# Token halves inside the passes: the order of the token-stationary matrix products in a four-layer model kernel

## What is computed

```
x = first_block(x, ...)    # 2 layers: three mixers, then an expert layer (PEER, 16384 experts)
  u   = rms_norm(x) @ w_in                       # 1024 -> 3462 columns
  x   = x + concat(hgrn2, dilated attention, mamba2) @ w_out
  q   = rms_norm(x) @ w_query
  x   = x + sum over the chosen experts of gate * gelu(down @ x) * up
x = second_block(x, mem, ...)   # 2 layers
  p   = rms_norm(x) @ w_in_2                     # 1024 -> 5888 columns
  x   = x + (gated sum of conv @ w_a_out, retention @ w_b_out, gating @ w_c_out) @ w_o
  x   = x + cross_attention(rms_norm(x), mem; xa_q, xa_k, xa_v, xa_o)
  x   = x + (silu(h @ w1) * (h @ w3)) @ w2       # 2816 inner columns
return rms_norm(x) * final_norm
```

## Time and profile before

| | |
|---|---|
| median of 3 runs | 3015.52 us |
| lowest and highest | 3012.93 and 3020.16 us |
| span of the profiled execution | 3015.1 us |
| mean granted TensorE clock, of full speed | 0.991 |
| TensorE matmul busy | 2947.5 us, 98% of the span |
| VectorE busy | 2016.0 us, 67% |
| ScalarE busy | 1456.8 us, 48% |
| mean DMA rate | 175 GB/s |

### The profile page before, as it was taken

One profiled execution on the slowest core, in us unless ns is written; L12 is line 12 of the kernel. 1 busy time (PEld: TensorE's weight loads), 2 busy tenths in 40 slices (PEclk: granted clock), 3 DMA queues, 4 the chain that ended last, 5 costly groups with the idle time before them and its releaser, 6 DMA issues.

```text
span 3015.1 us, 43968 instructions
## 1 busy us (share of the span) xinstructions
PE 2947.5 (98%) x17320; PEld 2604.2 (86%) x17320; DVE 2016.0 (67%) x3109; ACT 1456.8 (48%) x2275; POOL 14.9 (0%) x37
## 2 busy tenths in 40 slices
PE   8989999999999999999999999999999999999998
PEld 6878888889999788888888999988898998888996
DVE  5859998765555686889885655547665556665554
ACT  5531775554444444157645444435455444545443
POOL 0000000000000000000000000000000000000000
PEclk9999999999999999999999999999999999999999
DMA  5334446775545433444568554546555656554563
GB/s 178 109 113 153 168 168 209 249 268 183 195 178 181 136 99 112 148 163 169 200 224 292 193 196 169 197 141 181 179 171 169 189 187 186 170 182 146 150 187 125
DMA packets 223246, 528.52 MB, mean 175 GB/s; under 512 B 13450, under 2 KB 87344, under 8 KB 212080
## 3 DMA queue, kind: packets, MB, share of 16 engines
q1 hardware_dynamic: 221856, 521.11, 52.1%
q0 software_dynamic: 1232, 5.25, 0.5%
HBM read 507.42 MB, written 18.88 MB: 175 GB/s over the span
## 4 chain that ended last, share of the span: by engine, by line
PE 93%; DVE 4%; ACT 2%; DMA 1%; issue 0%; SPq 0%; POOL 0%; DVEq 0%; ACTq 0%; POOLq 0%
PE ps L2211 16%; PE ps L1232 14%; PE ps L2195 12%; PE ps L1282 12%; PE ps L1295 12%; PE ps L1266 11%; PE ps L559 4%; PE ps L550 3%; PE ps L1221 2%; PE ps L2452 1%; PE ps L653 1%; PE ps L1047 1%; DVE ring_lo L533 0%; PE ps L2376 0%; PE ps L2360 0%; PE ps L1207 0%
## 5 line engine op out<-in xcount | busy, mean ns | idle before, releaser
L1869 DVE TENSOR_TENSOR ring_lo<-ring,w_hi 128x1024 fp32r<-128x1024 f32 x320 | 388.8, 1224 | 272.2 <-ACT w_hi L1865 270.9
L1865 ACT ACTIVATE w_hi<-ring 128x1024 fp32r<-128x1024 f32 x320 | 336.7, 1057 | 270.5 <-PE ps L2211 183.9
L1232 PE MATMUL ps<-h_t,ring 128*128 128x256 f32 x2048 | 463.8, 379 | 1.1 <-ACT arena L882 0.9
L1232 PEld LDWEIGHTS ps<-h_t,ring 128*128 128x128 f32 x2048 | 378.9, 190 | 48.1 <-issue 1.3
L1282 PE MATMUL ps<-h_t_lo,down_hi 128*128 128x256 f32 x1024 | 288.2, 281 | 0.0
L1282 PE MATMUL ps<-h_t_expert,down_lo 128*128 128x256 f32 x1024 | 287.8, 281 | 0.0
L1282 PE MATMUL ps<-h_t_expert,down_hi 128*128 128x256 f32 x1024 | 286.8, 280 | 0.0
L2195 PE MATMUL ps<-h_t_hi,w_hi 128*128 128x256 f32 x928 | 259.9, 280 | 2.7 <-ACT arena L2010 2.7
L2195 PE MATMUL ps<-h_t_lo,w_hi 128*128 128x256 f32 x928 | 261.5, 282 | 0.0
L2195 PE MATMUL ps<-h_t_hi,ring_lo 128*128 128x256 f32 x928 | 259.7, 280 | 0.0
L1656 DVE TENSOR_TENSOR up_lo<-ring,up_hi 128x2048 fp32r<-128x2048 f32 x64 | 146.7, 2292 | 101.4 <-ACT up_hi L945 101.4
(11 more groups left out here) (442 smaller groups left out, 6700.2 us busy)
## 6 DMA issues: line engine op xcount, KB each, us to landing
ring<-in_peer_down SPq DMA_DIRECT2D x128, 1024.0 KB, 5.1
ring<-in_w_in SPq DMA_DIRECT2D x140, 512.0 KB, 3.6
ring<-in_peer_up SPq DMA_DIRECT2D x68, 1024.0 KB, 4.8
ring<-in_w SPq DMA_DIRECT2D x132, 512.0 KB, 3.7
ring<-in_peer_up SPq DMA_DIRECT2D x120, 512.0 KB, 4.1
arena<-late_gates SPq DMA_DIRECT2D x16, 1024.0 KB, 7.0
ring<-in_w_out SPq DMA_DIRECT2D x16, 512.0 KB, 3.5
ring<-in_peer_w_query SPq DMA_DIRECT2D x16, 512.0 KB, 3.5
```

The source lines that it names most:

```text
L1232: m = pe.e.matmul(PS[:, act_bank(b), j * T:(j + 1) * T], RING[:, b % 2, j * D + kc * P:j * D + (kc + 1) * P], HT[:, kc, :], start=kc == 0, ...
L1865: a.e.activation(W_HI[:, g % HI_SLOTS, :], RAW[:, g % RAW_SLOTS, :], ACT.Copy).then_inc(*a.count(f"c{g}_hi"))
L1869: v.e.tensor_tensor(RAW_LO[:, g % RAW_SLOTS, :], RAW[:, g % RAW_SLOTS, :], W_HI[:, g % HI_SLOTS, :].bitcast(F32), ALU.subtract).then_inc(* ...
```

## The change

In each of the three places the loop over the token halves becomes the innermost one. The products, their operands, their banks, the flags on the first and last one of a sum, the wait ahead and the signal behind are as before; only their order inside a chunk is new. The sums into one bank keep their order among themselves.

```diff
@@ front_chunk @@
-                for t in range(TT):
-                    o = slice(t * P, (t + 1) * P)
-                    for kc in range(k):
-                        for i, (z, y) in enumerate(((x[0], hi), (x[0], lo), (x[1], hi))):
-                            m = pe.e.matmul(PS[:, 2 * (j % 2) + t, 0:w], z[:, k * n + kc, o], y[:, kc, :],
+                for kc in range(k):
+                    for i, (z, y) in enumerate(((x[0], hi), (x[0], lo), (x[1], hi))):
+                        for t in range(TT):
+                            m = pe.e.matmul(PS[:, 2 * (j % 2) + t, 0:w], z[:, k * n + kc, t * P:(t + 1) * P], y[:, kc, :],
                                             start=n == 0 and kc == 0 and i == 0, stop=n == last and kc == k - 1 and i == 2)
@@ tokens, and the same in branch @@
-                for t in range(TT):
-                    o = slice(t * P, (t + 1) * P)
-                    for kc in range(2):
-                        for i, (y, w) in enumerate(((x[0], hi), (x[0], lo), (x[1], hi))):
-                            m = pe.e.matmul(PS[:, bank + t, :], y[:, k0 + kc, o],
+                for kc in range(2):
+                    for i, (y, w) in enumerate(((x[0], hi), (x[0], lo), (x[1], hi))):
+                        for t in range(TT):
+                            m = pe.e.matmul(PS[:, bank + t, :], y[:, k0 + kc, t * P:(t + 1) * P],
                                             w[:, kc, :], start=first and kc == 0 and i == 0,
                                             stop=last and kc == 1 and i == 2)
```

More of the change, by code:

```diff
@@ L2447, in branch @@
             hi, lo = chunk_view(g, 512, W_HI[:, g % HI_SLOTS, :]), chunk_view(g, 512, RAW_LO[:, g % RAW_SLOTS, :])
[L2448 to L2453, removed]
+            for kc in range(2):
+                for i, (y, w) in enumerate(((x[0], hi), (x[0], lo), (x[1], hi))):
+                    for t in range(TT):
+                        m = pe.e.matmul(PS[:, bank + t, :], y[kc][:, t * P:(t + 1) * P], w[:, kc, :],
+                                        start=first and kc == 0 and i == 0, stop=last and kc == 1 and i == 2)
             m.then_inc(*pe.count(f"c{g}_mm"))
```

## The result

| | before | changed |
|---|---|---|
| median of the runs (lowest to highest) | 3015.52 us (3012.68 to 3020.16), 7 runs | 3023.61 us (3020.28 to 3028.01), 7 runs |
| ratio, 95% interval | | 1.0023, 1.0013 to 1.0032 |
| span of the profiled execution | 3015.1 us | 3021.8 us |
| mean granted clock of it | 0.991 | 0.990 |

The changed kernel is slower by 0.23%, some 8 us. I had forecast 3011 us; the time lies inside the range, on the side to which I had given 0.21.

A forecast was written before the change was run, and what follows sets the result against it. TensorE's product-to-product rhythm was taken as the bound. Terms of -3.6, -0.9, +0.4 and -0.1 us gave -4.2, taking 3015.1 to 3010.9; with 0.4 for the runs' median, 3011 us, range 2994 to 3028.

The forecast's parts named there:

- What bounds the kernel: Whole span: TensorE carries 93% of the chain, so how fast it goes from product to product sets the end.
- distance = duration - 163: TensorE products: a median duration minus 163 ns gives the distance to the next start, within 1 ns.
- The wait and the signal: At the three changed places: waits ahead and the signal on the last product stay, so other engines see no difference; cost nothing.
- what is late next: In the `w2` stretch: ScalarE and VectorE have slack, so a TensorE 1 to 7% faster stays covered.
- The bank: Changed products: the bank changes at each product instead of each sixth; taken as costing nothing.
- rival 4: Changed products: switching banks each time makes TensorE pause and lose its clock; +64 us, 3079 us; chance 0.03.
- The stationary operand: Changed products: each load now differs from its neighbours, where one of three was a repeat; taken as costing nothing.
- The moving operand: Changed products: fewer changes of moving tile, so four of six distances were put at the cheap third pass; -4.2 us.
- term of -4.2 us: All three places: -3.6 us L2211 with `h_t`, -0.9 L559 of 512 columns, +0.4 `ff`, -0.1 L2452.
- Rival 3: Changed products: the second half's load disturbs the stream, all streams taking 398 ns; +12.6 us, 3028 us; chance 0.20.
- point of decision: Mean duration of changed products, 395.6 ns against 393.4 before, beyond which the slowdown exceeds 0.2%.
- signs that I named: Checks: `w_hi` medians with `h_t` to 388 to 392, 264 products within 0.3 us of 61.32; wrong if mean moves over 4 ns.

The follow-up runs named there:

- halves between: Kernel before with the loop over token halves moved between slices and passes, so the bank changes each third product: 3014.99 us, 0.9995.
- one bank for six: Changed kernel with both halves adding into one bank chosen by the slice, changing each sixth product; sums not the model's: 3023.34 us, 1.0021.
- slices innermost: Kernel before with slices and passes exchanged: halves outermost, then passes, then slices of channels: 3024.41 us, 1.0022.
- halves on different slices: Changed kernel with halves still alternating at each product, but the second half working on the other slice of channels: 3021.7 us, 1.0015.
- high columns four times: Changed kernel with passes reordered to hi·hi, lo·hi, hi·lo, so the high weights move four times in a row: 3018.93 us, 1.0008.
- two halves of the front alone: Two runs, kernel before with the changed order only in front chunks j >= 8, then only j < 8: 3018.6 us, 1.0004, and 3015.66 us, 1.0000.

## Why the prediction was wrong, and where it was right

The cause of the longer rhythm can be put in one table, the six distances that make up the cycle of a chunk (medians in ns at full clock, with `ff` from the 44 chunks of the two stretches of 264, with `h_t` from the 12 chunks of the stretch of 144):

```
with ff                            mean
before            236 228 229 233 233 233   232.0
halves between    236 228 229 233 233 233   232.0
changed           235 225 237 238 231 234   233.3
one bank for six  235 225 237 238 231 234   233.3
slices innermost  236 224 238 237 232 233   233.3
with h_t
before            233 224 229 233 224 229   228.7
halves between    233 224 229 233 224 229   228.7
changed           238 233 231 231 234 239   234.3
one bank for six  238 233 231 231 234 239   234.3
slices innermost  238 233 231 231 234 239   234.3
```

In these stretches two orders of tiles give two cycles, repeated within 1 or 2 ns over hundreds of products, whatever the bank and the half. The stretch of 144 shows the largest difference: over all products with `h_t` the means are 230.7 and 233.3. Nor has an order one cycle only. In the stretch at 2121.56 the kernel before runs at 236, 232 and 225 ns, the three distances that I had read from the medians; the changed one has a second cycle too, of 236, 231, 233, 233, 231 and 229 ns, and which of the two a stretch gets can differ between executions of the same program (22.34 and 22.56 us above).

- **What bounds the kernel, and that distance = duration - 163: right.** The chain stayed TensorE's, the loss shows alike in starts and in durations, and nearly all of it lies on the path. By the means it is 1344 x 2.6 + 528 x 1.1 + 192 x 0.8 (`mt`) + 192 x 0.5 (`branch`) = 4.3 us in the second block, where its length rose by 3.8. The 163 holds for the means; for a single product the difference lies between 158 and 165 ns.
- **The wait and the signal, what is late next: right.** The earlier trace rows and its counterpart are the same.
- **The bank: right.** Taking the alternation away from the changed kernel gave 3023.34 us; alternating by threes gave 3014.99. The granted clock is 1.00 in the changed `w2` stretch, so rival 4 did not come. The Trainium skill ("TensorE: Matmul & The Clock Gate", section "A second HAM failure mode: psum-queue depth-cycling") tells of a clock that oscillates when banks are cycled through with small idle times between the groups. This gapless stretch has no such idle times, 62.00 us busy of 62.00, so it neither bears the rule out nor speaks against it.
- **The stationary operand: right as far as tested.** Slices innermost loses the repeated load as the changed kernel does, but reordering the passes with the halves outermost loses it too, at 61.32 us for the 264.
- **The moving operand: this is the step that failed.** I read the third pass's 388 as the price of "the next product moves columns of the same tile" and put it for four of the six distances. In the changed kernel those four are the first, third and fifth of the cycle (inside the pairs) and the sixth (to the next slice): 238, 231, 234 and 239 ns with `h_t`, where I had 225. The two changes of tile, 233 and 231, were near what I had (235 and 231). Even the kernel before contradicts the reading: in its own stretch of 144 the distances are 233, 224 and 229, and the cheap one is behind the pass over `ring_lo`, where the tile changes. The medians of the earlier trace rows mix such cycles and hide this. So the 225 was never a property of one neighbourhood; it belonged to the whole cycle of three. The term of -4.2 us for the three places was, by the same means, +4.3 in the second block and (232.1 - 230.0) x 480 = +1.0 in the front.
- **Rival 3 had the sign and not the mechanism.** It blamed the second half's load under the stream. Slices innermost has no second half in its six and is as slow. Its point of decision was 395.6 ns, 2.2 more than before. The medians of all changed rows, weighted, come to 395.6 (396.0 with `h_t`, 396.7 with `ff`, 397.3 with `mt`, 393.7 with `branch`, 393.3 in the front), the distances to 1.9 more than before: about at the point, and the time lies just past 0.2%, with the clock's help. Without a mechanism that holds, that agreement is luck. The 398 in every row did not come.
- **Not in my sum: the clock of the front.** Some 2 us of the 8 go with 0.0009 less of granted clock over the runs. The runs whose whole front has the new order or another new one had means of 0.9899 to 0.9902 in six cases, but halves on different slices had 0.9909, the halves between 0.9915, the high columns four times and the changed kernel with the 64-byte pad had 0.9911, and the two halves of the front alone cost nothing that can be measured. The kernel before with a 32-byte pad had 0.9899 with its front unchanged. Whether the change lowers the clock, and through which products, stays open; so does what is left of the 8 us, which lies within the interval.
- **The signs that I named were in part too wide.** The `w_hi` medians with `h_t` went to 396 and 398 and not to 388 to 392, which shows that I was wrong. But the limit of 4 ns for the mean and that of 0.3 us for the 264 products would have let it pass: they moved by 1.9 ns and 0.29 us. And the sentence that this trace agrees with 216 ns for plain float32 doesn't hold: 216.4 is the distance at 256 plain columns, and the 512 plain ones of L1207, by my own rule, are at 429.

What stays open underneath is why a given order of tiles is dear. The place of the tiles has a part in it, as the pads show, but none of the rules on addresses tested above fits all the shifts, and what picks one of an order's cycles is not shown.

## What to carry to other kernels

In a gapless stretch of reduced-precision products the order of the operand tiles and their place in SBUF moved the rhythm by 0.5 to 2.5% here. A median of one pass can't be carried over to a new order, because the distances belong to the cycle as a whole, and it may mix two cycles: look at single starts in one stretch first. Alternating two banks at each, each third or each sixth product made no difference. Before crediting a few microseconds to an edit, compare at an equal granted clock and look at stretches that the edit doesn't touch: here a front without the edit ended 3.6 us later in one execution than in another (221.08 and 217.50 us), nearly as much as the edit costs.

## What the runs showed of the hardware that I had not expected

- Products of one kind, width and format are 224 to 240 ns apart, in cycles of three or six that repeat over a stretch. None came to 216 ns, the rhythm of L1232, though the same columns moved two and four times in a row. The figure of 216 for N = 512 in the Trainium skill ("TensorE: Matmul & The Clock Gate", section "Back-to-back issue gap") was seen in none of these orders.
- The same program can run the same stretch in either of two cycles: 96 products of the changed kernel took 22.34 us in one execution and 22.56 in another.
- A pad of 32 bytes took the expert products from 390 or 391 ns to 389 for all three passes (5.9 us over two stages), and the same `ff` stretch took 61.02 us in one layer and 61.62 in the next of the same program.
- The length of the first front is not a constant of the code: the first experts began at 217.29 us with slices innermost, 220.47 in the changed kernel and 222.39 with the halves between, whose rhythm is that of the kernel before. The time in it at low clock was 13.7, 23.9 and 27.3 us, in that order.
